# One core, a transformer block with product-key experts: the last eight modulation sums stand in other chunks of the expert phase, and the blocks of the gate matrix G are spread over fewer halves

## The chip, the core and the metric

The kernel runs on one core of a Trainium2 chip, in one launch. The metric is the device time of that launch in microseconds (us); of several runs the median counts.

## What is computed

The program runs two blocks on 256 tokens of width 1024. The change lies in the expert layer of the first block and in one of the vectors that it is gated with:

```python
def adaln_params(cond, w_mod, b_mod):
    mod = jax.nn.silu(cond) @ w_mod + b_mod
    return mod.reshape(cond.shape[0], N_MOD, 1, cond.shape[-1])
...
        u = expert_u[experts]
        vsel = expert_v[experts]
        act = jax.nn.gelu(jnp.einsum('thkd,td->thk', u, hb), approximate=False)
        return jnp.einsum('thk,thkd->td', gate * act, vsel)
...
        x = x + mod[:, 5] * peer_ffn(h2, peer_w_query[layer], peer_sub_keys[layer], peer_u[layer], peer_v[layer])
```

There are 16,384 experts, and each token chooses 8 x 16 of them. The kernel gathers nothing: it multiplies all tokens with all experts, and a matrix G, with the gate of each pair of token and expert (zero where the token did not choose the expert), weighs the result before the second product.

## The kernel before

**Chunks and halves.** All large weights come as 257 chunks of 1 MB, one after the other, into three buffers `raw`. A chunk has two halves of 128 x 1024. Each half is split in two fp32r parts: ScalarE (ACT) copies it to `w_hi`, VectorE (DVE) subtracts to get `w_lo` (a helper records both, at lines 1399 and 1827), and TensorE (PE) multiplies three times with the pair (line 868). There are four slots for pairs, and both ACT and DVE split up to three halves ahead of the one that PE is to start (`ahead`). SyncE (SP) issues in one queue, in program order: chunk n only when both halves of chunk n-3 have been read by DVE.

**The expert phase.** 64 chunks U and 64 chunks V. First come U(0) to U(35), 72 halves h = 0 to 71, alone. Then a loop over c = 0 to 63 runs V(c), and from c = 34 to 61 U(c+2) ahead of it. U(c) is finished by a gelu on ACT. Before V(c), DVE multiplies the gelu's result by G (`weigh(c)`, output `wfull`), ACT rounds that to `HC` (`w_high`), DVE makes the rest (`weighed_low`, again `HC`). DVE's iteration c is: `weighed_low(c+1)`, splits of U(c+2) if there is one, `weigh(c+2)`, a split, `one_hots` of block 36+c (for c < 28), a modulation sum if it stands here, a split.

**G's blocks.** G is made in two rounds of 32 blocks of 8 tokens. For block n DVE writes one-hot rows (`one_hots(n)`, five operations, after PE has finished block n-2), PE multiplies them (`g_block(n)`, 24 matmuls of 128x64), ACT copies the result (`g_copy(n)`). The first round, blocks 0 to 31, runs beside the U halves: NG = 42, so they follow the halves h = 30 to 71, block 31 right after the last half. `weigh(0)` needs all 32 of them. Blocks 32 and 33 follow the last half, and block 34+c stands at V(c) for c < 30. Block 32 may be copied only once `weigh(0)` has read G, block 33 after `weigh(1)`.

**The eight modulation sums.** The vector mod[:, 5] is made of the blocks 40 to 47 (`GATE2`). Each is one operation on DVE over 128x1024 (`mod_block`, line 1984) on a piece of `w_mod` of 0.5 MB that lies in `x`, which is free at that time. `gate2_at(n)` says in which c it stands: 28, 30, ..., 42. SP asks for the piece of block n ahead of the chunk V(c) of that c (lines 835 to 837); as there is one buffer, it first waits until the sum of block n-1 is done (`summed`), and whatever stands behind in SP's queue waits too. V(28) is chunk 96, V(30) chunk 98; from c = 34 on there are two chunks for each c. The finished vector is turned by PE at c = 48, goes through DRAM and is read in the norm behind V(63); `x` is brought back from DRAM from chunk V(48) on.

**Reloads.** The gelu results of U(8) to U(35) are kept in DRAM and reloaded one for each V chunk (0.25 MB, lines 847 and 855). SP waits for the landing of one before it issues the next.

Of the kernel before, what the change touches and what calls it, by code (L numbers as in the profile page):

```python
# [28 lines left out]
NBL = 256 // TB  # L29
# [58 lines left out]

NU = 36
NG = 42  # L90


KEPT = range(8, NU)
# [3 lines left out]
def blocks_after(h):  # L97

    j = h - (2 * NU - NG)
    return range(NBL * j // NG, NBL * (j + 1) // NG) if j >= 0 else range(0)  # L100

PEER_U, PEER_V = {}, {}

# [135 lines left out]

def gate2_at(n):  # L240

    return 28 + 2 * (n - GATE2[0])


def mod_issue():


    at, u = {}, 0
    for s in FRONT:
        if s in HALF_OF:  # L250
            u = HALF_OF[s]
        elif s[0] == "mod":
            at[s] = u
    out, chunk = {}, 0
    for n in range(NMOD, GATE2[0]):
        before = HALF_OF["win", 0, 2] if n < NMOD + 4 else at["mod", n - 4]
        chunk = max(chunk, (before + 9) // 2)
        out.setdefault(chunk, []).append(n)
    for n in GATE2:
        out.setdefault(PEER_V[gate2_at(n)] // 2, []).append(n)  # L260
    return out


# [124 lines left out]
def program(nc, wall, keys_d, cols_d, rows_d, bigrows_d, crow_d, wmod_d, dist_d, x_d, ctx_d, pT_d, gws_d, out_d, n_chunks):  # L388
    assert n_chunks * 2 == U_END
    with ExitStack() as es:  # L390
# [409 lines left out]
        def sync_program(e):  # L800
            e.dma_start(cols[:, :], cols_d).then_inc(s_tab, 16)
            e.dma_start(crow_ctx, crow_d[1024:2048].partition_broadcast(128)).then_inc(s_crow, 16)
            e.dma_start(crow, crow_d[0:1024].partition_broadcast(128)).then_inc(s_crow, 16)
            for n in range(n_chunks):
                if n == 1:
                    e.dma_start(x[:, :, :], x_d.rearrange("(i p) d -> p i d", p=128)).then_inc(s_x, 16)
                if n == 2:
                    e.dma_start(ctx, ctx_d.rearrange("(i p) d -> p i d", p=128)).then_inc(s_ctx, 16)
                if n == 6:
                    e.dma_start(rows[:, :], rows_d.partition_broadcast(128)).then_inc(s_tab, 16)  # L810
                if n == 10:
                    e.wait_ge(s_tab, 32)
                    e.dma_start(dist, dist_d.rearrange("p (a b) -> p a b", a=4)).then_inc(s_tab, 16)
                if n == 11:
                    e.wait_ge(s_c2, 3)
                    e.dma_start(crow_keep.rearrange("(p d) -> p d", p=1), crow[0:1, :]).then_inc(s_ckeep, 16)
                if n == U_QUERY // 2:
                    e.wait_ge(s_pt_, 8)
                    e.dma_start(skeep, keys_d).then_inc(s_keys, 16)
                if n == U_QUERY // 2 + 4:  # L820
                    e.wait_ge(s_res, result(N_PEER, 1, 1))
                    e.dma_start(x_keep, x[:, :, :].rearrange("p i d -> p (i d)")).then_inc(s_xkeep, 16)
                if n == PEER_V[48] // 2:
                    e.wait_ge(*summed(GATE2[7]))
                    e.dma_start(x[:, :, :].rearrange("p i d -> p (i d)"), x_keep).then_inc(s_xback, 16)
                for m in MOD_ISSUE.get(n, []):
                    place, times = mod_slot(m)
                    if m < NMOD + 4:
                        e.wait_ge(*summed(7))
                        e.wait_ge(s_std, 2)  # L830
                    elif m == GATE2[0]:
                        e.wait_ge(s_w, 24)
                        e.wait_ge(s_ckeep, 16)
                        e.dma_start(crow2, crow_keep.partition_broadcast(128)).then_inc(s_rawm[4], 16)
                    else:
                        e.wait_ge(*summed(m - (1 if m in GATE2 else 4)))
                    e.dma_start(mod_raw[place], wmod_d[m - NMOD]).then_inc(s_rawm[place], 16)
                if n >= NRAW:
                    for u in (2 * (n - NRAW), 2 * (n - NRAW) + 1):
                        e.wait_ge(*read(u))  # L840
                e.dma_start(raw[:, n % NRAW, :], wall[n]).then_inc(s_raw[n % NRAW], 16)
                if n in ACTS_OUT:
                    c = ACTS_OUT[n]
                    e.wait_ge(s_gelu, c + 1)
                    if c > KEPT[0]:
                        e.wait_ge(s_ao, kept(c - 1))
                    e.dma_start(act_keep[c - KEPT[0]], act_made(c)).then_inc(s_ao, 16)
                if n in ACTS_IN:
                    c = ACTS_IN[n]
                    e.wait_ge(s_ao, kept(KEPT[-1]))  # L850
                    if c > KEPT[0]:
                        e.wait_ge(s_ai, kept(c - 1))
                    if c >= KEPT[4]:
                        e.wait_ge(s_w, c - 3)
                    e.dma_start(act_of(c), act_keep[c - KEPT[0]]).then_inc(s_ai, 16)
            for i in range(2):
                for hf in range(2):
                    s_ = slice(hf * 512, (hf + 1) * 512)
                    e.wait_ge(s_fin, 2 * i + hf + 1)
                    e.dma_start(out_d[i * 128:(i + 1) * 128, s_], gt[:, i, s_]).then_inc(s_out, 16)  # L860
            e.wait_ge(s_out, 64)


        def tensor_program(e):
# [333 lines left out]
            for h in range(2 * NU):  # L1198
# [3 lines left out]
                    turn_choice(1, sel)  # L1202
                for b in blocks_after(h):
                    g_block(b)
            for b in (NBL, NBL + 1):
                g_block(b)
            for c in range(64):
                if NU <= c + 2 < 64:
                    for m in range(2):
                        u_half(c + 2, m)  # L1210
                if c == 48:
                    t.wait_ge(s_gc, NQ * NBL)
                    gate_turned(GATE2[0])
                if NBL + 2 + c < NQ * NBL:
                    g_block(NBL + 2 + c)
                if c < 62:
                    for m in range(2):
                        for i in range(2):
                            ins = tok_half(PEER_V[c] + m, i, [0, 1, 2, 3], lambda i: weighed(c, m, i), c == m == 0, False)
                        t.did(ins, s_used)  # L1220
# [168 lines left out]
        def scalar_program(e):  # L1389
# [252 lines left out]
            def w_high(c):  # L1642
                a.wait_ge(s_w, c + 1)
                if c >= 2:
                    a.wait_ge(s_used, used(PEER_V[c - 2] + 1))
                act(WR[:, c % 2, 0, :], wfull, ACT.Copy, sig=s_wh)

            for h in range(2 * NU):
# [8 lines left out]
                        act(gsel, gsel, ACT.Exp, sig=s_ge)  # L1657
                for b in blocks_after(h):
                    g_copy(b)
            w_high(0)  # L1660
            for b in (NBL, NBL + 1):
                g_copy(b)
            for c in range(64):
                if c < 63:
                    w_high(c + 1)
                if NU <= c + 2 < 64:
                    for m in range(2):
                        ahead(PEER_U[c + 2] + m)
                    a.wait_ge(s_w, c + 1)
                    gelu(c + 2)  # L1670
                if c < 63:
                    ahead(PEER_V[c])
                if NBL + 2 + c < NQ * NBL:
                    g_copy(NBL + 2 + c)
                if c < 62:
                    ahead(PEER_V[c] + 1)
                if c == 48:
                    a.wait_ge(s_gtn, 2)
                    act(gT, PB[6][0:8, 0:128], ACT.Copy, sig=s_gcp)
            norm(N_F1, PEER_V[63] + 1, f_scr)  # L1680
# [139 lines left out]
        def vector_program(e):  # L1820
# [470 lines left out]
            def weighed_low(c):  # L2291
                v.wait_ge(s_wh, c + 1)
                tt(WR[:, c % 2, 1, :], wfull, WR[:, c % 2, 0, :].bitcast(F32), SUB, sig=s_wl)
# [3 lines left out]
            for h in range(2 * NU - NG, 2 * NU):  # L2297
                for b in blocks_after(h - 1):
                    one_hots(b + 2)
                ahead(U_PEER + h)  # L2300
            for b in blocks_after(2 * NU - 1):
                one_hots(b + 2)
            weigh(0)
            weighed_low(0)
            weigh(1)
            for n in range(NBL + 2, NBL + 4):
                one_hots(n)
            mods_at = {gate2_at(n): n for n in GATE2}
            for c in range(64):
                if c < 63:  # L2310
                    weighed_low(c + 1)
                if NU <= c + 2 < 64:
                    for m in range(2):
                        ahead(PEER_U[c + 2] + m)
                if c + 2 < 64:
                    weigh(c + 2)
                if c < 63:
                    ahead(PEER_V[c])
                if NBL + 4 + c < NQ * NBL:
                    one_hots(NBL + 4 + c)  # L2320
                if c in mods_at:
                    mod_block(mods_at[c])
                if c == 46:
                    added_mods(GATE2[0], 48)
                if c < 62:
                    ahead(PEER_V[c] + 1)
# [390 lines left out]
```

## Time and profile before

| | us |
|---|---|
| median of three runs | 1788.83 |
| the three runs | 1788.52 to 1795.13 |
| the profiled execution, its own time | 1793.46 |
| its span, first to last instruction | 1791.7 |
| PE busy | 1666.4 (93%) |
| DVE busy | 1254.2 (70%) |
| ACT busy | 909.8 (51%) |

Below, a row of a timeline gives the start, the duration, the engine and the operation, and in square brackets how long the engine had stood idle before it and what ended that. A row can stand for several operations in a row (x5), and small gaps lie in its duration. PE is shown busy until the modelled end of a matmul, so its pace is read from the starts of rows that come again, not from its busy share. The granted clock is 1 at 2.4 GHz and 0.5 at 1.2 GHz. The expert phase ends near 1153 us.

### The profile page before, as it was taken

The page shows a single profiled execution, that of the slowest core. Times are in us where ns is not written, and L with a number is a line of the kernel's source. Part 1 is how long each engine was busy: PE and PEld are TensorE (multiplying, and loading weights), DVE is VectorE, ACT ScalarE, POOL GpSimd, SP SyncE. Part 2 cuts the span into 40 slices and gives each one's busy share as a digit, 9 for nine tenths or more (in the row PEclk, how much of TensorE's full clock was granted, in tenths as well). Part 3 has the DMA queues.
Part 4 walks back from the last instruction along what each step waited for, and adds up shares of the span by engine and source line. Part 5 has one row for each costly group of instructions (what it writes and reads, how often), then busy time and mean ns, then how long its engine had stood idle before and what let it go on. Part 6 is the DMA issues. An engine that isn't in the chain of part 4 may idle for free.

```text
span 1791.7 us, 29060 instructions
## 1 busy us (share of the span) xinstructions
PE 1666.4 (93%) x11518; PEld 1492.9 (83%) x11518; DVE 1254.2 (70%) x2040; ACT 909.8 (51%) x1206; POOL 84.2 (5%) x50
## 2 busy tenths in 40 slices
PE   6898787999999899988999999999998888999996
PEld 6676566998999788867999999899998777899995
DVE  5886655899888899976666555665556885655555
ACT  3454445554555455534444444544446766544445
POOL 1100002622000000000000000000000000000000
PEclk9898888999999999999999999999999998999998
DMA  6743333446655355637555555454543532555541
GB/s 262 275 168 133 106 110 123 144 165 200 205 182 199 141 201 202 220 133 267 211 199 211 198 189 186 154 200 177 191 185 130 212 130 106 190 193 188 188 171 64
DMA packets 53418, 318.52 MB, mean 178 GB/s; under 512 B 5953, under 2 KB 6113, under 8 KB 19362
## 3 DMA queue, kind: packets, MB, share of 16 engines
q1 hardware_dynamic: 52098, 310.60, 48.7%
q0 software_dynamic: 1184, 6.05, 0.9%
q8 instruction: 91, 1.49, 0.3%
q14 instruction: 45, 0.37, 0.1%
HBM read 307.17 MB, written 9.47 MB: 177 GB/s over the span
## 4 chain that ended last, share of the span: by engine, by line
PE 61%; DVE 25%; ACT 10%; issue 2%; DMA 2%; DVEq 0%; SPq 0%; ACTq 0%
PE pb L868 60%; DVE w_lo L1827 7%; DVE ar L1827 7%; ACT w_hi L1399 4%; ACT ar L1399 3%; DVE ar L1839 2%; DMA raw<-in_wall 1%; DVE HC L1827 1%; DVE ar L2181 1%; ACT L1399 1%; ACT HC L1399 1%; DVE ar L2178 1%; DVE ar L1984 1%; DVE raw L1984 1%; DVE ar L1981 1%
## 5 line engine op out<-in xcount | busy, mean ns | idle before, releaser
L1827 DVE TENSOR_TENSOR w_lo<-raw,w_hi 128x1024 fp32r<-128x1024 f32 x467 | 572.3, 1225 | 277.3 <-ACT w_hi L1399 251.8
L868 PE MATMUL pb<-HX,w_hi 128*128 128x256 f32 x3904 | 716.7, 285 | 12.2 <-DVE w_lo L1827 10.7
L1399 ACT ACTIVATE w_hi<-raw 128x1024 fp32r<-128x1024 f32 x498 | 528.2, 1061 | 346.2 <-PE pb L868 297.9
L868 PEld LDWEIGHTS pb<-HX,w_hi 128*128 128x128 f32 x3904 | 614.0, 193 | 19.7 <-DVE w_lo L1827 10.3
L868 PE MATMUL pb<-HX,w_lo 128*128 128x256 f32 x1952 | 553.9, 284 | 0.0
L868 PE MATMUL pb<-w_hi,HC 128*128 128x512 f32 (+1 forms) x1648 | 530.8, 393 | 11.7 <-DVE HC L1827 11.2
L868 PEld LDWEIGHTS pb<-HX,w_lo 128*128 128x128 f32 x1952 | 375.9, 193 | 0.0
L868 PEld LDWEIGHTS pb<-w_hi,HC 128*128 128x128 f32 x1648 | 312.0, 190 | 76.4 <-DVE w_lo L1827 12.5
L868 PE MATMUL pb<-w_lo,HC 128*128 128x512 f32 (+1 forms) x824 | 322.4, 391 | 0.0
L1827 DVE TENSOR_TENSOR ar<-ar 128x512 bf16<-128x512 bf16 (+8 forms) x470 | 247.5, 563 | 59.3 <-ACT ar L1399 30.9
L1399 ACT ACTIVATE ar<-pb 128x512 f32<-128x512 f32 (+3 forms) x203 | 112.7, 555 | 242.6 <-PE pb L868 154.9
L868 PE MATMUL pb<-w_hi,HX 128*128 128x512 f32 x512 | 177.7, 416 | 13.2 <-DVE w_lo L1827 5.6
L868 PEld LDWEIGHTS pb<-w_lo,HC 128*128 128x128 f32 x824 | 156.6, 190 | 29.4
L868 PE MATMUL pb<-ar 128*128 128x64 bf16 (+3 forms) x1960 | 134.1, 228 | 26.4 <-DVE ar L1827 8.7
L868 PEld LDWEIGHTS pb<-ar 128*128 128x128 bf16 (+2 forms) x1960 | 111.7, 124 | 50.7 <-issue 26.8
L868 PEld LDWEIGHTS pb<-w_hi,HX 128*128 128x128 f32 x512 | 102.4, 200 | 38.2 <-issue 11.4
L1399 ACT ACTIVATE HC<-ar 128x512 fp32r<-128x512 f32 x87 | 55.0, 632 | 103.8 <-PE pb L868 60.7
L868 PE MATMUL pb<-w_lo,HX 128*128 128x512 f32 x256 | 104.4, 408 | 0.0
L1827 DVE TENSOR_TENSOR HC<-ar,HC 128x512 fp32r<-128x512 f32 x87 | 60.3, 693 | 46.6 <-ACT HC L1399 42.8
L2565 POOL TENSOR_TENSOR w_lo<-raw,w_hi 128x1024 fp32r<-128x1024 f32 x31 | 75.7, 2442 | 158.5 <-ACT w_hi L1399 117.9
L1399 ACT ACTIVATE ar<-ar 128x512 f32<-128x512 f32 (+7 forms) x85 | 50.3, 591 | 57.5 <-DVE ar L1839 23.8
L868 PEld LDWEIGHTS pb<-w_lo,HX 128*128 128x128 f32 x256 | 51.3, 201 | 9.7
(139 smaller groups left out, 716.1 us busy)
## 6 DMA issues: line engine op xcount, KB each, us to landing
raw<-in_wall SPq DMA_DIRECT2D x257, 1024.0 KB, 4.8
ar<-in_wmod SPq DMA_DIRECT2D x24, 512.0 KB, 3.7
act_keep<-ar SPq DMA_DIRECT2D x28, 256.0 KB, 5.6
ar<-act_keep SPq DMA_DIRECT2D x28, 256.0 KB, 5.1
x<-in_wmod SPq DMA_DIRECT2D x8, 512.0 KB, 3.3
ar<-in_bigrows POOLq DMA_DIRECT2D x2, 1024.0 KB, 5.1
ar<-acs_keep POOLq DMA_DIRECT2D x2, 1024.0 KB, 8.4
ar<-in_crow SPq DMA_DIRECT2D x2, 512.0 KB, 5.9
```

The lines of the kernel that those rows point to most:

```text
L868: return e.matmul(o, l, r, start=start, stop=stop, skip_group_check=True)
L1399: a.did(e.activation(out, in_, func, scale=scale, **kw), sig)
L1827: v.did(e.tensor_tensor(out, a_, b_, op), sig)
L1839: v.did(e.scalar_tensor_tensor(out, a_, s_, b_, op0, op1), sig)
L1981: v.did(e.scalar_tensor_tensor(junk, w, 1.0, crow_ctx, MUL, MUL, accum_out=modT[:, n, 1:2]))
L1984: v.did(e.scalar_tensor_tensor(w, w, 1.0, c_, MUL, MUL, accum_out=modT[:, n, 0:1]), s_modv)
L2178: v.did(e.max(vals[:, c_], src))
L2181: v.did(e.max_index(idx[:, c_], vals[:, c_], src))
L2565: p.did(e.tensor_tensor(w_lo[:, made % NH, :], raw_half(w), w_hi[:, made % NH, :].bitcast(F32), SUB), s_lop)
```

## The change

Three things change.

1. `gate2_at` gives c = 34, 36, ..., 48 in place of 28, 30, ..., 42, and the piece of block n is asked for one chunk later than V(c)'s own (in the chunk of U(c+3), which follows V(c)). What hangs on the last sum moves by six: the bias is added at c = 52 (46 before), the turn stands at c = 54 (48), `x` comes back from V(54) on.
2. Blocks 0 to 31 are spread over 38 halves in place of 42, h = 30 to 67. The halves 68 to 71 have none of them.
3. Work that stood behind the last U half stands beside it: `weigh(0)` at h = 69, `weighed_low(0)`, `weigh(1)`, `one_hots(34)`, `w_high(0)` and the blocks 32 and 33 at h = 70. `one_hots(35)` follows h = 71.

```diff
+U_LAST = 2 * NU - 1
...
-    return range(NBL * j // NG, NBL * (j + 1) // NG) if j >= 0 else range(0)
+    return range(min(NBL, NBL * j // (NG - 4)), min(NBL, NBL * (j + 1) // (NG - 4))) if j >= 0 else range(0)
...
-    return 28 + 2 * (n - GATE2[0])
+    return 34 + 2 * (n - GATE2[0])
...
-        out.setdefault(PEER_V[gate2_at(n)] // 2, []).append(n)
+        out.setdefault(PEER_V[gate2_at(n)] // 2 + 1, []).append(n)
...
-                if n == PEER_V[48] // 2:
+                if n == PEER_V[54] // 2:
...
-            for b in (NBL, NBL + 1):
-                g_block(b)
+                if h == U_LAST - 1:
+                    for b in (NBL, NBL + 1):
+                        g_block(b)
...
-                if c == 48:
+                if c == 54:
                     t.wait_ge(s_gc, NQ * NBL)
                     gate_turned(GATE2[0])
...
-            w_high(0)
-            for b in (NBL, NBL + 1):
-                g_copy(b)
+                if h == U_LAST - 1:
+                    w_high(0)
+                    for b in (NBL, NBL + 1):
+                        g_copy(b)
...
-            for b in blocks_after(2 * NU - 1):
-                one_hots(b + 2)
-            weigh(0)
-            weighed_low(0)
-            weigh(1)
-            for n in range(NBL + 2, NBL + 4):
-                one_hots(n)
+                if h == U_LAST - 2:
+                    weigh(0)
+                if h == U_LAST - 1:
+                    weighed_low(0)
+                    weigh(1)
+                    one_hots(NBL + 2)
+            one_hots(NBL + 3)
...
-                if c == 46:
+                if c == 52:
                     added_mods(GATE2[0], 48)
```

SP's queue in the stretch V(28) to V(33), before: a piece of `w_mod` (`in_wmod`) ahead of chunks 96, 98, 100 and 103. `in_wall` is a chunk, `act_keep` a reload.

```order
L834 DMA x<-crow_keep 128x1024
L837 DMA x<-in_wmod 128x1024
L841 DMA raw<-in_wall 128x2048
L855 DMA ar<-act_keep 128x512
L841 DMA raw<-in_wall 128x2048
L855 DMA ar<-act_keep 128x512
L837 DMA x<-in_wmod 128x1024
L841 DMA raw<-in_wall 128x2048
L855 DMA ar<-act_keep 128x512
L841 DMA raw<-in_wall 128x2048
L855 DMA ar<-act_keep 128x512
L837 DMA x<-in_wmod 128x1024
```

The same queue now, from chunk 100 on:

```order
L842 DMA raw<-in_wall 128x2048
L856 DMA ar<-act_keep 128x512
L842 DMA raw<-in_wall 128x2048 x2
L856 DMA ar<-act_keep 128x512
L835 DMA x<-crow_keep 128x1024
L838 DMA x<-in_wmod 128x1024
L842 DMA raw<-in_wall 128x2048 x4
L838 DMA x<-in_wmod 128x1024
L842 DMA raw<-in_wall 128x2048 x4
```

The first piece now stands ahead of chunk 104, behind the last reload, and each next one four chunks on.

DVE at the end of the U halves, before. `ar<-ar 128x512` followed by `128x1024` and three more `128x512` is one `one_hots`; a `128x512` more is a `weigh`; `HC` is `weighed_low`.

```order
L1827 TENSOR_TENSOR w_lo<-raw,w_hi 128x1024
L1827 TENSOR_TENSOR ar<-ar 128x512
L1827 TENSOR_TENSOR ar<-ar 128x1024
L1827 TENSOR_TENSOR ar<-ar 128x512 x4
L1827 TENSOR_TENSOR HC<-ar,HC 128x512
L1827 TENSOR_TENSOR ar<-ar 128x512 x2
L1827 TENSOR_TENSOR ar<-ar 128x1024
L1827 TENSOR_TENSOR ar<-ar 128x512 x4
L1827 TENSOR_TENSOR ar<-ar 128x1024
L1827 TENSOR_TENSOR ar<-ar 128x512 x3
L1827 TENSOR_TENSOR HC<-ar,HC 128x512
```

DVE there now, from the splits at h = 68 and 69 on:

```order
L1830 TENSOR_TENSOR w_lo<-raw,w_hi 128x1024 x2
L1830 TENSOR_TENSOR ar<-ar 128x512
L1830 TENSOR_TENSOR w_lo<-raw,w_hi 128x1024
L1830 TENSOR_TENSOR HC<-ar,HC 128x512
L1830 TENSOR_TENSOR ar<-ar 128x512 x2
L1830 TENSOR_TENSOR ar<-ar 128x1024
L1830 TENSOR_TENSOR ar<-ar 128x512 x3
L1830 TENSOR_TENSOR w_lo<-raw,w_hi 128x1024
L1830 TENSOR_TENSOR ar<-ar 128x512
L1830 TENSOR_TENSOR ar<-ar 128x1024
L1830 TENSOR_TENSOR ar<-ar 128x512 x3
L1830 TENSOR_TENSOR HC<-ar,HC 128x512
```

The two `weigh` and the first `weighed_low` now have three splits among them, and the last split before V(0) stands between `one_hots(34)` and `one_hots(35)`. No operation is added or taken away on any engine.

## Rows read from the trace of the kernel before

**Rows 1.** The chain that ended last, in time: start, us, what
```profile
786.41 5.43 DMA raw<-in_wall
```
**Rows 2.** Stretches: us, busy PE, PEld, DVE, ACT, POOL; PE clock, DMA share, GB/s
```profile
588.00:598.00 10.00, 4.05 (x101) 3.83 (x100) 8.55 (x17) 4.71 (x7) 0.00 (x0) 0.82 0.26 104
...
780.00:830.00 50.00, 37.03 (x177) 29.85 (x175) 28.58 (x32) 17.65 (x21) 0.00 (x0) 0.90 0.53 205
...
795.00:799.00 4.00, 3.88 (x9) 3.13 (x10) 3.16 (x4) 2.91 (x4) 0.00 (x0) 0.50 0.08 24
...
812.00:816.00 4.00, 3.35 (x9) 2.66 (x10) 3.69 (x4) 3.03 (x4) 0.00 (x0) 0.62 0.87 309
```
**Rows 3.** Timeline of V(28) to V(33), DVE and SP
```profile
781.78 0.69 DVE L1827 TENSOR_TENSOR HC<-ar,HC 128x512 fp32r<-128x512 f32 x1
...
784.72 1.23 DVE L1984 SCALAR_TENSOR_TENSOR x<-x 128x1024 f32<-128x1024 f32 x1
...
785.98 0.33 SPq L837 DMA_DIRECT2D x<-in_wmod  x1
...
792.55 0.33 SPq L855 DMA_DIRECT2D ar<-act_keep  x1
```
**Rows 4.** Timeline of PE, V(28) to V(34)
```profile
776.13 0.47 PE L868 MATMUL pb<-w_hi,HC 128*128 128x512 f32 x1
...
781.70 0.90 PE L868 MATMUL pb<-ar 128*128 128x64 bf16 x24
782.62 0.47 PE L868 MATMUL pb<-w_hi,HC 128*128 128x512 f32 x1
...
795.12 0.77 PE L868 MATMUL pb<-w_hi,HC 128*128 128x512 f32 x1 [6.82 <-DVE HC L1827]
...
812.65 0.51 PE L868 MATMUL pb<-w_hi,HC 128*128 128x512 f32 x1 [4.41 <-DVE HC L1827]
...
830.10 0.50 PE L868 MATMUL pb<-HX,w_hi 128*128 128x256 f32 x2 [1.82 <-DVE w_lo L1827]
...
833.07 0.40 PE L868 MATMUL pb<-w_hi,HC 128*128 128x512 f32 x1
```
**Rows 5.** Waits from 832 to 1160 us: engine <- releaser: total us, times, longest
```profile
PE pb L1078 <- DVE x L1827: 2.6, 3, 1.5
```
**Rows 6.** Timeline of PE, U halves with a block after them
```profile
542.75 0.90 PE L868 MATMUL pb<-ar 128*128 128x64 bf16 x24
...
549.33 0.90 PE L868 MATMUL pb<-ar 128*128 128x64 bf16 x24
...
553.02 0.90 PE L868 MATMUL pb<-ar 128*128 128x64 bf16 x24
```
**Rows 7.** Timeline of DVE, U halves 67 to 71
```profile
576.29 1.23 DVE L1827 TENSOR_TENSOR w_lo<-raw,w_hi 128x1024 fp32r<-128x1024 f32 x1 [1.19 <-ACT w_hi L1399]
578.18 2.16 DVE L1827 TENSOR_TENSOR ar<-ar 128x512 bf16<-128x512 bf16 x5 [0.67 <-PE pb L868]
...
585.57 2.16 DVE L1827 TENSOR_TENSOR ar<-ar 128x512 bf16<-128x512 bf16 x5 [0.21 <-PE pb L868]
```
**Rows 8.** Timeline of PE and DVE, last U half to V(1)
```profile
588.33 1.63 PE L868 MATMUL pb<-ar 128*128 128x64 bf16 x48
...
591.52 0.89 PE L868 MATMUL pb<-ar 128*128 128x64 bf16 x24 [1.57 <-DVE ar L1827]
...
596.79 1.44 PE L868 MATMUL pb<-ar 128*128 128x64 bf16 x24 [4.38 <-DVE ar L1827]
598.04 0.77 PE L868 MATMUL pb<-w_hi,HC 128*128 128x512 f32 x1
...
599.05 0.69 DVE L1827 TENSOR_TENSOR HC<-ar,HC 128x512 fp32r<-128x512 f32 x1
...
605.85 0.47 PE L868 MATMUL pb<-w_hi,HC 128*128 128x512 f32 x1
...
605.97 0.69 DVE L1827 TENSOR_TENSOR HC<-ar,HC 128x512 fp32r<-128x512 f32 x1 [0.51 <-ACT HC L1399]
```

More of the change, by code:

```diff
@@ L1676, in scalar_program @@
                     ahead(PEER_V[c] + 1)
-                if c == 48:
+                if c == 54:
                     a.wait_ge(s_gtn, 2)
```

## Prediction

> **What bounds the kernel now.** I read the chain of waits first, then the busy time by stretches, then the timelines around each place where PE stands idle. PE is busy 93% of the span, so only the places where it is not can give time back. In the expert phase there are two.
>
> The first is V(28) to V(34). In the 50 us from 780 PE is busy 37.03 us, at a mean clock of 0.90 [rows 2]. It stands idle 6.82 us ahead of V(30), 4.41 ahead of V(32) and 1.82 inside U(36) [rows 4]. The chain runs there through a chunk's transfer that starts at 786.41 and takes 5.43 us [rows 1]. SP's queue tells why it starts so late: the sum of block 40 ends near 786, and at 785.98 SP issues the next piece of w_mod, with chunk 98 right behind [rows 3]. Without that wait, chunk 98 would have been issued when chunk 95 was read, and that is over two V chunks earlier. So the wait for a sum, which stands in front of a chunk in an in-order queue, is what holds PE. Behind 832 us PE waits on nothing but three short waits of the norm's rows, 2.6 us in all [rows 5], although five of the eight sums stand there.
>
> The second is the step from U to V. The last U half ends at 588.33; PE then does blocks 31 and 32, waits 1.57 us, does block 33, waits 4.38, does block 34 and starts V(0) at 598.04 [rows 8], in a stretch where it is busy 4.05 of 10 us [rows 2]. What it waits for is DVE, which has `weigh(0)`, `weighed_low(0)`, `weigh(1)` and two `one_hots` to do one after the other.
>
> **Pace of PE and DVE between them.** A U half with a block takes 553.02 - 549.33 = 3.69 us, two halves with one block 549.33 - 542.75 = 6.58; so a half is 2.89 and a block 0.80 [rows 6]. V(1) starts at 605.85 [rows 8] and V(28) at 776.13 [rows 4]: 170.28 / 27 = 6.307 us a chunk, without idle time. DVE's `weighed_low(2)` starts at 605.97 [rows 8] and `weighed_low(29)` at 781.78 [rows 3]: 175.81 / 27 = 6.511. DVE is the slower one by 0.204 a chunk, but starts with a lead. `weighed_low(c+1)` may start up to 5.65 us after V(c) (781.78 - 776.13); at c = 1 it starts 0.12 after, at c = 28 the lead is gone, and V(29) starts at 782.62, as soon as `weighed_low(29)` is done (781.78 + 0.84). The start of V(29) is therefore set by PE and by DVE at once: moving PE's start of V alone would gain nothing. The transition is worth what DVE gains.
>
> **Part 1, the step from U to V.** PE: the last U half now has blocks 31, 32 and 33 ahead of it in addition, 3 x 0.80, and ends at 590.7; block 34 follows, and V(0) could start at 591.5, 6.5 earlier than now. DVE: counting back from 590.7 by halves of 2.89 and two blocks, U half 69 ends at 583.3 on PE. ACT then does a gelu (0.6) and the copy of half 73 (1.06; both from the durations of its line on the page), so DVE gets that half at 585.0, and this is its last wait. What it then has to do, with a gap of 0.10 behind each (split 1.23 and `one_hots` 2.16 in [rows 7], `weighed_low` 0.69 in [rows 8], and `weigh` of the same shape): split 1.33, `weighed_low(0)` 0.8, `weigh(1)` 0.8, `one_hots(34)` 2.26, split 1.33, `one_hots(35)` 2.26, together 8.8. `weighed_low(1)` starts at 593.8 (599.05 now), and one iteration of 6.51 later `weighed_low(2)` at 600.3 against 605.97. DVE gains 5.7 us. At c = 1 it is 600.3 - 597.8 = 2.5 behind V(1), so its lead is used up near c = 1 + (5.65 - 2.5) / 0.204 = 16, and from there it paces. V(29) starts at 600.3 + 27 x 6.511 + 0.84 = 776.9 in place of 782.62. **5.7 us** gained, of the 6.5 plus the slow first 3 us of V(0) that PE alone would have.
>
> Where does DVE's time come from? Halves without a block cost it 1.19 + 0.67 = 1.86 us of waiting, halves with one 0.21 [rows 7]. Four of ten such halves go from the spread to the end, and there `weigh` and the rest stand in them. That the blocks are closer costs PE nothing: a half with a block is 3.69 us for PE and 1.33 + 2.26 = 3.59 for DVE.
>
> **Part 2, the sums.** From V(29) to V(34) there are now 833.07 - 782.62 = 50.45 us [rows 4]. The work in it is five V chunks without a block, 776.13 to 781.70, thus 5.57 each, and the two halves of U(36): 27.85 + 5.8 = 33.6. The rest, 16.8 us, is 13.05 of idle time and 3.8 of matmuls at the lower clock behind it (795 to 799 stands at 0.50, the 1.2 GHz level, 812 to 816 at 0.62) [rows 2]. With no piece asked for in that stretch SP is held by nothing but reads. DVE needs 2 x 1.33 + 2 x 0.8 = 4.3 us a chunk there against PE's 5.57, and so gets its lead back. **16.8 us** gained.
>
> The Trainium skill ("TensorE: Matmul & The Clock Gate", Part 1) says that the array is throttled by default and activity releases it, and that the penalty is the throttled time times one minus the ratio. An estimate by that page from the granted clock of the two stretches is 3.88 x 0.50 + 3.35 x 0.38 = 3.2 us in place of my 3.8, and the sum would be 0.6 smaller.
>
> **What the moved sums cost where they now stand.** Eight sums of 1.33 us lie beside U and V chunks, one in each second c. There DVE has 4 splits, `weigh`, `weighed_low` and a sum in 11.3 us of PE: 5.3 + 1.6 + 1.3 = 8.2. The five that stand there already cost PE nothing [rows 5]. The request for a piece is in front of chunk 104 + 4i, and the sum it waits for is done when DVE has read chunk 100 + 4i and before it reads 101 + 4i; chunk 104 + 4i can't be issued before 101 + 4i is read, so SP never waits for the sum where it counts. A piece has four chunks to land. Queued behind that request are its own chunk and nothing else, the reloads having ended with chunk 102. The copy of the row and the piece, 1 MB in all, come before chunk 104, once. Turn, way through DRAM and return of `x` start six c later, with nine c (100 us) left to the norm: 0. Nothing in `gate2_at` touches POOL but through that turn.
>
> **Sum.** 5.7 + 16.8 = 22.5 us. The profiled execution, 1793.46, would become 1771.0; it stands 4.6 above the median of the runs, which would become 1788.83 - 22.5 = **1766.3**.
>
> **Rivals.**
>
> B, DVE gains nothing at the step. Its margin in the U halves is 0.1 us a half (3.59 against 3.69). If the closer blocks make it late, V(29) stays where it is, and only part 2 is left: 1788.8 - 16.8 = 1772.0. For it: two values 3% apart. Against: six light halves stay among the 38, each with 1.86 us to catch up.
>
> C, the reloads pace V(28) to V(33). SP waits for one to land before it issues the next; between about 786.9, right behind the chunk of [rows 1], and the next issue at 792.55 [rows 3] lie 5.67 us, and with 0.45 for issuing 6.1 against PE's 5.57. Six chunks would give back 3.2 us: 1769.5. Against: that transfer shared the queue with a piece and two chunks, and DVE and the buffers are two chunks ahead. The mean of 205 GB/s at a share of 0.53 [rows 2] means that 237 GB/s (1.31 MB in 5.57 us) fill 0.61 of the engines.
>
> D, the sums stall the mixed stretch (slower). Seven requests wait for the sum before them. Three cost 16.8 us where they were, 5.6 each; if a sum came later than the read of the chunk before by more than a chunk's spare time, some 5 us, seven would cost 39, and the time would be 1766.3 + 39 = 1805. Against it stands [rows 5]: the same requests one chunk earlier cost nothing.
>
> E, the 13 us idle have a second cause (a reload or buffer that comes late anyway). Then only part 1 is left: 1788.8 - 5.7 = 1783.1.
>
> F, PE sets V's pace throughout, because DVE comes out earlier than I count: V(29) at 597.8 + 28 x 6.307 = 774.4, 8.2 gained at the step: 1763.8.
>
> **Numbers.** Forecast 0.68, B 0.12, C 0.08, D 0.03, E 0.04, F 0.05. The range reaches from F less 1.5 of spread among runs to B with the same, 1762 to 1773.5. Half a per cent is 8.9 us, about what a measurement of this kernel can tell from no change: faster by more are the forecast, B, C and F, 0.93; E is within it, 0.04; D is slower, 0.03.
>
> **What would show it.** In the profile of the changed kernel: V(0) within 1 us of the last U half, at full clock; `weighed_low(2)` near 600; PE's V chunks 6.31 apart up to about V(16) and 6.51 apart behind it, up to V(29) near 777; no idle time over 1 us from there to V(34), which starts near 810 in place of 833.07; SP's waits for a sum with no PE wait beside them. The prediction is wrong if PE waits behind a block in the halves 30 to 71, if V(30) to V(33) are over 5.7 apart, or if a wait for a split stands near a sum.

## Result and profile after

The changed kernel takes 1774.4 us in the median of four runs (1771.53 to 1776.26), and the kernel before, in four runs of which three are the ones above, 1791.98 (1788.52 to 1796.58). The ratio is 0.9889, with a 95% interval of 0.987 to 0.9908. Put on the 1788.83 that I started from, that is 1769.0 us (1765.6 to 1772.4); the median itself lies 0.9 us above the range of 1762 to 1773.5, because more runs moved the kernel before up from 1788.8 to 1792, and to 1793.9 to 1795.4 in the later comparisons. Forecast was a gain of 22.5 us; the three comparisons of the changed kernel give 19.9, 21.0 and 21.4, and the span of the profiled execution fell by 21.9, from 1791.7 to 1769.8.

The page of the changed kernel, the chain that ended last:

```profile
PE 73%; DVE 17%; ACT 7%; issue 1%; DMA 1%; SPq 0%; DVEq 0%; ACTq 0%
```

Busy times are what they were (PE 1665.2 us, DVE 1254.4, ACT 910.0); PE's share of the chain that ended last has grown to 73% (61% on the page of before), and that of the DMA has fallen to 1% (2%).

The step from U to V, timeline of PE, which answers to [rows 8]:

```profile
582.89 1.63 PE L869 MATMUL pb<-ar 128*128 128x64 bf16 x48
...
587.31 0.90 PE L869 MATMUL pb<-ar 128*128 128x64 bf16 x24
588.04 0.48 PE L869 MATMUL pb<-w_hi,HC 128*128 128x512 f32 x1
```

Blocks 32 and 33 stand ahead of the last U half, block 34 right behind it, V(0) behind that, at full clock (0.48 and not 0.77 us for its first matmul) and without a wait. The same place on DVE, its `weighed_low(1)` and `(2)`:

```profile
590.70 0.69 DVE L1830 TENSOR_TENSOR HC<-ar,HC 128x512 fp32r<-128x512 f32 x1
...
597.22 0.69 DVE L1830 TENSOR_TENSOR HC<-ar,HC 128x512 fp32r<-128x512 f32 x1
```

They are 6.52 us apart (6.92 in the kernel before, with the idle 0.51 of [rows 8], in which DVE waits for ACT). V(1) starts at 594.33, so DVE is 2.9 us behind it at c = 1 (2.5 forecast). How that goes on is seen in the chain, start, us and what:

```profile
579.93 109.26 PE pb L869 x890
689.27 6.46 PE pb L869 x48
...
773.96 257.59 PE pb L869 x1608
```

Up to 689 us, the end of V(15), PE is in one piece, at 6.31 us a chunk (V(15) itself starts 6.43 behind V(14)); behind that each V chunk is a piece of its own, 6.52 us apart, and starts when its `weighed_low`, 5.68 us behind the start of the chunk before, is done; and from V(29) on, at 773.96, the chain is PE alone for 257 us. In the kernel before a chunk's transfer stood in that place [rows 1].

The stretches that answer to those of [rows 2], same columns, the V(29) to V(34) stretch in the second:

```profile
586.00:596.00 10.00, 10.00 (x92) 8.55 (x91) 9.20 (x18) 6.25 (x8) 0.00 (x0) 1.00 0.35 101
773.00:823.00 50.00, 49.92 (x286) 43.35 (x286) 38.80 (x39) 27.00 (x30) 0.00 (x0) 1.00 0.70 249
```

PE is busy 49.92 of 50 us in place of 37.03, at clock 1.00 in place of 0.90, and the DMA engines move 249 GB/s at a share of 0.70. SP in the same stretch asks for its first piece at 791.89 and the second at 811.64, and no PE wait stands beside them. What SP waited for a sum from 770 to 1000 us, in all, times and longest, in the kernel before and in the changed one:

```profile
SPq L837 <- DVE x L1984: 65.5, 7, 19.7
```
```profile
SPq L838 <- DVE x L1987: 6.6, 7, 1.0
```

The seven waits are still there, but short. For all of 832 to 1160 us PE's waits are again three for the norm's rows, 2.6 us in all.

### The profile page after: what moved, and what is told of

Same layout as the page of the kernel before. It is cut to its first block, busy times and chain, and to the rows that moved or that the text cites. A ratio compares the mean times of both kernels' runs of the same rounds, so it can differ in the third digit from the quotient of the medians.

```text
span 1769.8 us, 29060 instructions
## 1 busy us (share of the span) xinstructions
PE 1665.2 (94%) x11518; PEld 1493.6 (84%) x11518; DVE 1254.4 (71%) x2040; ACT 910.0 (51%) x1206; POOL 84.7 (5%) x50
## 4 chain that ended last, share of the span: by engine, by line
PE 73%; DVE 17%; ACT 7%; issue 1%; DMA 1%; SPq 0%; DVEq 0%; ACTq 0%
PE pb L869 72%; DVE w_lo L1830 4%; DVE ar L1830 3%; ACT ar L1401 3%; DVE ar L1842 2%; ACT w_hi L1401 2%; DVE ar L2184 1%; ACT L1401 1%; DMA raw<-in_wall 1%; DVE ar L1987 1%; DVE ar L2181 1%; DVE raw L1987 1%; DVE ar L1984 1%; ACT HX L1401 1%; DVE ar L2188 0%
## 5 line engine op out<-in xcount | busy, mean ns | idle before, releaser
L869 PE MATMUL pb<-w_hi,HC 128*128 128x512 f32 (+1 forms) x1648 | 525.3, 390 | 2.3 <-DVE HC L1842 1.2
```

The source lines that it names most:

```text
L869: return e.matmul(o, l, r, start=start, stop=stop, skip_group_check=True)
```

## Experiments

All numbers of the next table are starts read from the profiled execution's timeline of PE. T is the last of the six matmuls that turn the chosen experts, ahead of the first block; what the expectations call the end of the queries is this point, 0.54 us behind the start of their row. The last column is a stage of the second block that no edit touches, from PE's matmul 9000 to 10000 of 11518.

| kernel | T to V(0) | V(0) to V(1) | V(1) to V(29) | V(29) to V(34) | V(34) to V(48) | untouched stage |
|---|---|---|---|---|---|---|
| before | 159.5 | 7.8 | 176.8 | 50.4 | 157.1 | 201.9 |
| before_again | 158.0 | 7.3 | 176.9 | 50.5 | 157.1 | 203.6 |
| after | 151.4 | 6.3 | 179.6 | 33.0 | 157.1 | 206.0 |
| after_again | 152.9 | 6.3 | 179.5 | 33.1 | 157.1 | 203.4 |
| after_third | 151.4 | 6.3 | 179.6 | 33.0 | 157.1 | 205.9 |
| mods_only | 158.0 | 7.2 | 177.0 | 33.0 | 157.1 | 203.7 |
| blocks_only | 151.4 | 6.3 | 179.6 | 51.4 | 157.3 | 203.8 |
| ask_later | 158.0 | 7.3 | 176.8 | 33.2 | 157.1 | 203.7 |
| ask_early | 151.4 | 6.3 | 179.5 | 33.0 | 174.6 | 205.5 |
| spread_only | 155.7 | 8.4 | 176.7 | 51.8 | 157.1 | 203.6 |
| pool_five | 152.9 | 6.3 | 182.8 | 33.0 | 157.1 | 199.4 |
| fuller | 152.9 | 6.3 | 176.8 | 33.0 | 157.1 | 203.6 |

**before_again and after_again: what two traces of one kernel differ by.** No edit.

> The kernel before, unchanged, against itself. Theory (run spread): the ratio is 1.000 and its interval tells what can be told apart, some 3 us either way. In its profile the stretch from V(29) to V(34) takes 50.4 us again (50.45 in the first trace) and V(0) to V(29) 184.6 again, within 0.5, since they are set by waits that don't depend on the clock's phase; the front (up to 440 us) and the mixer behind 1340 us may differ by 2 to 5 us, because the granted clock falls at other places there. Rival (the change did something behind 1340 us): those two differ by under 1 us between two traces of the same kernel, and then the 4 us that the changed kernel gave back between 1345 and 1490 us are its own.

> The changed kernel, unchanged. Ratio 0.988 to 0.990 again. In its profile V(0) starts within 1 us of the last U half, V(29) to V(34) takes 33.0 us within 0.3, PE's V chunks are 6.31 us apart up to about V(14) and 6.51 behind it. Theory (run spread): the stage behind 1340 us comes out 1 to 4 us other than in the first trace of the changed kernel. Rival (the change costs something there): it is as long as in the first trace, within 0.5 us.

Ratios 0.9996 (0.9986 to 1.0005) and 0.9883 (0.9869 to 0.9897). V(29) to V(34) came again within 0.1 us in both kernels. The untouched stage took 201.9 and 203.6 us in two traces of the kernel before and 206.0, 203.4 and 205.9 in three of the changed kernel. One kernel's own traces thus differ there by up to 2.6 us, less than the 4 us that the changed kernel seemed to give back behind 1340 us; but before_again and after_again have 203.6 and 203.4, and among all traces of the table, in which this stage has the same code, it takes 199.4 to 206.0. The 4 us are no effect of the change, and the rival falls. The stretch in after and in after_again, as busy time by stretch:

```profile
1316.00:1522.00 206.00, 188.67 (x1002) 161.96 (x1001) 146.43 (x213) 130.57 (x182) 4.31 (x7) 0.92 0.40 147
```
```profile
1320.00:1524.00 204.00, 184.58 (x1004) 158.00 (x1004) 146.49 (x214) 131.01 (x182) 4.32 (x7) 0.94 0.41 150
```

The longer one has the lower clock, 0.92 against 0.94, and 4.1 us more of busy PE, with the same DVE and ACT work. The 1.5 us by which T to V(0) differs between after and after_again are of that kind too: the 40 us from 441 have a mean clock of 1.00 in the one and those from 443 a mean of 0.96 in the other.

**mods_only: part 2 alone.** The kernel before with

```diff
-    return 28 + 2 * (n - GATE2[0])
+    return 34 + 2 * (n - GATE2[0])
...
-        out.setdefault(PEER_V[gate2_at(n)] // 2, []).append(n)
+        out.setdefault(PEER_V[gate2_at(n)] // 2 + 1, []).append(n)
```

and what hangs on it at 54 and 52.

> Only the sums are moved (c = 34 to 48, asked for one chunk on); the blocks and the step from U to V are as before. Theory (SP's wait for a sum holds the chunks): V(29) starts where it does in the kernel before, V(29) to V(34) takes 33.0 us in place of 50.4, gain 17.4 us, ratio 0.990. Rival (the two parts are not additive, the sums' stretch would need DVE's lead from the other part): DVE comes into V(28) with no lead here as in both kernels, so the gain would be under 14 us, with PE waits of over 1 us ahead of V(30) or V(31).

V(29) to V(34) took 33.04 us, 17.4 less; ratio 0.9912 (0.9898 to 0.9927), 15.8 us (13 to 18). DVE has no lead at V(28) here either, and PE did not wait. The first theory holds.

**blocks_only: part 1 and the spread alone.** The changed kernel with the lines of mods_only turned back.

> Only the blocks and the step from U to V are changed; the sums stand at c = 28 to 42 and are asked for as before. Theory (the step is worth what DVE gains): V(0) starts about 10 us earlier than before relative to a common point in the U halves' beginning, but V(29) only 5.7 to 7 us earlier, the stretch V(29) to V(34) is 50.4 us again, ratio 0.9965. Rival (the two gains overlap, as DVE reaches V(28) just as late and the stall swallows the rest): under 3 us, ratio over 0.998. Rival (PE's start counts): 9 us or more.

T to V(29) took 337.2 us against 342.2 in before_again: 5.0 gained, as much as DVE gains (its `weighed_low(2)` starts 160.5 us behind T, 165.5 in before_again). V(0) comes 6.6 earlier, not about 10. At V(1) it is 7.7 (165.3 against 157.7), and 2.7 are given back up to V(29), because DVE then sets the pace. The stretch behind it took 51.35, 0.9 more, so 4.1 are left in the profile. Timed: 0.9985 (0.9977 to 0.9994), 2.7 us (1.1 to 4.1); the 0.9965 expected lies outside, and the number that came is that of the first rival (under 3 us, over 0.998). Its mechanism is not what the trace shows, for V(29) comes 5.0 earlier; but that was under the 5.7 to 7 expected, and not all of it passed the stall. Here is the stretch from V(29) to V(34) in before_again, in blocks_only and, of an experiment further down, in spread_only; in the changed kernel the same matmuls are busy 33.04 us, at clock 1.00:

```profile
782.25:832.73 50.48, 36.88 (x169) 30.52 (x170) 29.05 (x31) 18.75 (x21) 0.00 (x0) 0.90 0.56 214
```
```profile
775.62:826.97 51.35, 37.65 (x168) 31.37 (x169) 30.30 (x32) 18.74 (x21) 0.00 (x0) 0.90 0.57 220
```
```profile
779.82:831.60 51.78, 39.31 (x169) 32.60 (x169) 30.45 (x32) 18.74 (x21) 0.00 (x0) 0.87 0.57 219
```

PE's idle time is 13.6 us in before_again and 13.7 here. Nearly all of the 0.9 is in the matmuls themselves: at the waits the clock falls to its 1.2 GHz level for a while (0.50 from 795 to 799 us in [rows 2]), and how much work falls into that while differs (one trace each).

**ask_later: the sums stay, only the request moves.** One line of the kernel before:

```diff
-        out.setdefault(PEER_V[gate2_at(n)] // 2, []).append(n)
+        out.setdefault(PEER_V[gate2_at(n)] // 2 + 2, []).append(n)
```

> The kernel before with one edit: each piece is asked for two chunks later; the sums stay at c = 28 to 42. Theory (the in-order wait in SP's queue is the cause, not where DVE does the sums): the sum waited for is then done 1.3 us after the chunk could go anyway, so V(29) to V(34) takes 33.0 to 34.5 us in place of 50.4 (33.04 with the sums moved), ratio 0.991. DVE has the sum's 1.33 us in V(28), V(30), V(32) on top of 4.3 us, against PE's 5.45. Rival (the sums' own time on DVE, which reaches V(28) without a lead, holds PE): 3 x 1.3 us and more of waits stay, over 37 us. Rival (the piece lands too late for its sum): DVE waits for a piece ahead of a sum, and PE behind it.

V(29) to V(34) took 33.2 us, ratio 0.9904 (0.9886 to 0.9922). This one line gives what mods_only gives, and neither rival came. The timeline of DVE and SP around the first sum shows why:

```profile
785.02 1.22 DVE L1984 SCALAR_TENSOR_TENSOR x<-x 128x1024 f32<-128x1024 f32 x1
```
```profile
771.97 0.33 SPq L841 DMA_DIRECT2D raw<-in_wall  x1
...
778.47 0.33 SPq L841 DMA_DIRECT2D raw<-in_wall  x1
...
786.28 0.33 SPq L837 DMA_DIRECT2D x<-in_wmod  x1
786.71 0.38 SPq L841 DMA_DIRECT2D raw<-in_wall  x1
```

The sum ends and SP asks for the next piece as in [rows 3], but chunks 98 and 99 had left the queue ahead of the wait, at 771.97 and 778.47. In the kernel before both stood behind it. So it is neither the sum nor its place on DVE, but what stands behind the wait in SP's queue.

**ask_early: the same wait put back where the sums now are.** The changed kernel with

```diff
-        out.setdefault(PEER_V[gate2_at(n)] // 2 + 1, []).append(n)
+        out.setdefault(PEER_V[gate2_at(n)] // 2 - 2, []).append(n)
```

> The changed kernel with one edit: the pieces are asked for two chunks ahead of V(c), not one behind it; the sums stay at c = 34 to 48. Theory (a chunk queued behind a sum costs what the path chunk, copy, split, 8.7 us from the end of the sum, takes beyond what PE has split ahead, some 7.3 us in the mixed stretch): seven waits of about 1.4 us, V(34) to V(48) 157.1 + 10 = 167 us (160 to 180). V(29) to V(34) stays at 33.0. Rival (the mixed stretch is immune): 157.1 again.

V(34) to V(48) took 174.6 us, 17.5 more, in the range but above the 10 worked out; the one time was 1788.13 us. PE waited seven times for a split, 12.5 us in all. The first of the seven, on DVE, SP and PE:

```profile
809.95 1.23 DVE L1987 SCALAR_TENSOR_TENSOR x<-x 128x1024 f32<-128x1024 f32 x1
...
811.21 0.33 SPq L838 DMA_DIRECT2D x<-in_wmod  x1
...
818.27 1.23 DVE L1830 TENSOR_TENSOR w_lo<-raw,w_hi 128x1024 fp32r<-128x1024 f32 x1 [7.09 <-ACT w_hi L1401]
819.55 0.50 PE L869 MATMUL pb<-w_hi,HC 128*128 128x512 f32 x1 [1.60 <-DVE w_lo L1830]
```

From the end of the sum to PE's start are 8.4 us: issue, landing, copy, split. Five of the seven waits are as forecast (1.4 to 1.7, and 1.4 worked out); the fourth and the fifth are 2.6 and 2.4, as from the issue of the chunk to ACT's copy 6.5 and 6.3 us pass there and 5.6 in the first (811.63 to 817.18). What I had left out is what follows the waits: PE's busy time from V(34) to V(48) is 162.1 us in place of 157.1. Of these 5.0 us some 3.3 are the clock, which stands at 0.50 from 893.2 to 896.6 and from 920.5 to 923.9, at the two longest waits; the rest is 0.2 to 0.3 us behind each of the seven. So the intervals of two c are 22.44 us without a wait, 24.1 to 24.4 with a short one and 26.7 with each of these two.

**spread_only: the closer blocks without the rest.** The kernel before with the line of `blocks_after` alone.

> The kernel before with one edit: blocks 0 to 31 over 38 halves; the step from U to V stands behind the last half as before, and so do the sums. Theory (the step is worth what DVE gains, and DVE gains only if work stands in the halves that are left empty): from the end of the queries (438.4 us in the traces) to V(29) 342.2 us in the kernel before, 337.2 with both edits; here 2.4 less than 342.2, so 339.8. The ratio is 0.998 to 0.999. Rival (closer blocks alone give all of it): 337.2. Rival (they cost PE or DVE something in the U halves): over 342.2.

T to V(29) took 340.9 us, 1.3 less, and V(29) to V(34) 1.3 more, all of it in busy PE at a lower mean clock (the rows at blocks_only: PE idle 12.5 us there, busy 39.31); ratio 0.9995 (0.9985 to 1.0005). That V(29) would gain 2.4 was too much: V(0) comes 2.3 earlier but `weighed_low(2)` and V(1) only 1.2, and PE waits 3.8 us for `one_hots(34)`. Closer blocks mainly empty the last halves; most of the gain is in the work that is put there (3.7 of the 5.0 us).

**pool_five: taking five splits off DVE.** The changed kernel with

```diff
+LO_POOL |= {PEER_V[c] + 1 for c in (4, 8, 12, 16, 20)}
...
-            ahead(PEER_U[15] + 1)
+            ahead(PEER_V[20] + 1)
```

> The changed kernel with one edit: GpSimd (POOL) subtracts five of the V halves, the second ones of V(4), V(8), V(12), V(16), V(20), in place of DVE. Theory (DVE paces V(14) to V(29), at 6.51 us a chunk against PE's 6.307): DVE has 1.33 us less five times, more than the 3.0 us by which it falls behind, so the chunks are 6.31 us apart up to V(29), and from V(1) to V(29) it is 28 x 6.307 = 176.6 us in place of 179.6; the kernel is 3 us shorter, ratio to the kernel before 0.9866. Rival (POOL's subtraction, 2.4 us on the page, comes too late or slows DVE's operations beside it): waits of PE for POOL, 179.6 or more.

V(1) to V(29) took 182.8 us, 3.3 more; ratio 0.9894 (0.987 to 0.9918). The rival came true. Timeline of POOL and DVE at the first of the five:

```profile
614.23 1.23 DVE L1831 TENSOR_TENSOR w_lo<-raw,w_hi 128x1024 fp32r<-128x1024 f32 x1
614.29 3.42 POOL L2569 TENSOR_TENSOR w_lo<-raw,w_hi 128x1024 fp32r<-128x1024 f32 x1 [196.19 <-ACT w_hi L1402]
615.56 2.70 DVE L1831 TENSOR_TENSOR HC<-ar,HC 128x512 fp32r<-128x512 f32 x1
```

POOL's subtraction takes 3.42 us here and `weighed_low` beside it 2.70 in place of 0.69. DVE is spared 1.33 us and loses 2.01, and as `weighed_low` is what PE waits for, PE waits four times 1.3 us. The rows read as if the two engines took turns: in all five places POOL's subtraction ends 2.2 to 2.3 us after DVE's split beside it has ended (615.46 and 617.71 above), and `weighed_low` 0.5 to 0.6 us after POOL's (618.26). That reads as waiting, on both engines, and not as slower work. The Trainium skill ("GPSIMD Engine Reference", Specifications) says that GpSimd shares its SBUF interfaces with VectorE, with contention for DVE instructions that have two SBUF inputs; this one has two, and the trace agrees.

**fuller: more of DVE's work in the U halves.** The changed kernel with these lines; what goes with them on PE, on ACT and in DVE's loop over c is left out here:

```diff
-    return range(min(NBL, NBL * j // (NG - 4)), min(NBL, NBL * (j + 1) // (NG - 4))) if j >= 0 else range(0)
+    return range(min(NBL, NBL * j // (NG - 6)), min(NBL, NBL * (j + 1) // (NG - 6))) if j >= 0 else range(0)
...
-                if h == U_LAST - 2:
+                if h == U_LAST - 4:
                     weigh(0)
-                if h == U_LAST - 1:
+                if h == U_LAST - 3:
                     weighed_low(0)
                     weigh(1)
                     one_hots(NBL + 2)
-            one_hots(NBL + 3)
+                if h == U_LAST - 2:
+                    one_hots(NBL + 3)
+                if h == U_LAST - 1:
+                    weighed_low(1)
+                    weigh(2)
```

> The changed kernel carried on: blocks 0 to 31 over 36 halves, weigh(0) at h = 67, weighed_low(0), weigh(1), blocks 32 and 33 at h = 68, one_hots(35) at h = 69, and weighed_low(1), weigh(2) and w_high(1) at h = 70, so that more of DVE's work lies in the U halves, where it waits for PE, and weighed_low(2) can start with V(1). Theory (V(1) to V(29) takes 179.5 us in the changed kernel in place of 28 x 6.307 = 176.6 because DVE starts it with too small a lead): 176.6 to 177, V(0) no later in relation to the U halves, 3.0 us less in all; ratio to the kernel before 0.9865. Rival (DVE's pace in V is bound by something that a lead doesn't help): 6.51 us a chunk from V(14) on again. Rival (DVE becomes late in the U halves): PE waits for a split or a block between 450 and 588 us.

> The changed kernel once more, on the same chip as the version carried on. V(1) to V(29) 179.5 us, V(29) to V(34) 33.05, ratio 0.988.

V(1) to V(29) took 176.8 us, 2.8 less than in the changed kernel, so PE is its own bound up to V(28). T to V(0) is 152.9, as in after_again; the 1.5 more than in after_third are clock again (0.96 in the 40 us from 441). The times on one chip are 1769.25 us against 1773.46, ratios 0.9857 (0.984 to 0.9873) and 0.9881 (0.9864 to 0.9897). The intervals overlap; that it is faster rests on the 2.8 us of the trace and on four runs that all lie below the four of the other (1769.0 to 1769.5, 1772.8 to 1773.6). It is the best version of this study.

## Why the prediction was right, point by point

- **The wait in SP's queue.** Right, and shown from three sides: taken out with the sums moved (33.0 us), taken out with the sums in place (33.2), put back elsewhere (17.5 us lost). The gain was forecast at 16.8 and measured at 17.4, as V(29) to V(33) take 5.46 us each in the mean and not 5.57; my 5.57 was read from V(28), which follows a block. In the terms of my sum that is 13.05 of idle time and 4.4 of slower matmuls, not 3.8. By the rule on the clock's share from the Trainium skill ("TensorE: Matmul & The Clock Gate", Part 1) it would have been 16.2, further off. The fault there was my choice of two windows of 4 us: over all of the low clock in which PE works (795.12 to 799.28 and 812.94 to 816.35, 7.57 us at 0.50) an estimate by the same rule gives 3.8 in place of 3.2.
- **The step from U to V is worth what DVE gains.** Right in its mechanism: V(1) comes 7.7 us earlier, `weighed_low(2)` 5.0, and V(29) 5.0. The size was forecast at 5.7 (T to V(29) is 342.2 against 337.2). About half of the miss is DVE's end, 2.9 us behind V(1) and not 2.5. The other half is the trace I counted from, in which `weighed_low(2)` is 6.92 us behind `weighed_low(1)`, with 0.51 of idle time at a low clock [rows 8]; in before_again it is 6.51. The 1.5 us more of slow clock ahead of V(0) in that trace shift both ends of my sum alike.
- **The switch of the bound.** Forecast near V(16), seen at V(15); V(29) is set by DVE at 6.52 us a chunk. fuller shows that the lead is what was missing.
- **Moved sums cost nothing.** Right: 157.1 us in both kernels from V(34) to V(48).
- **Sum.** 5.0 + 17.4 = 22.4 in the traces against 22.5: the two misses, 0.7 too much and 0.6 too little, cancel, and that the sum comes out to 0.1 is luck. Timed it is 19.9 to 21.4, with intervals that reach from 16.5 to 24.4 and all hold 22.4.
- **Rivals.** Neither B nor F occurred, as the step gained 5.0 us, not 0 or 8.2; in fuller, another kernel, PE sets V's pace as F has it. C didn't occur: V(29) to V(33) follow each other at 5.44 to 5.52 us with the reloads in the queue. D's mechanism exists, but its price is 2.5 us a request in the mixed stretch (ask_early) and not the 5.6 that I took from the pure V chunks; I put that down to the U chunk more of split work that PE has there, which no run separates. E fell with mods_only.
- **The base.** The median of my three runs, 1788.83, was 5 us below what 23 runs gave later (1793.9), the single runs reaching from 1788.5 to 1797.6, and I took 1.5 us for the spread among runs. That, and not the mechanism, put the median of the changed kernel 0.9 us outside the range.

## What to carry to other kernels

A wait placed in front of a request in a queue that issues in order holds everything behind it: put the request as many places back as its data can spare, and the wait costs nothing, without moving any work (here two chunks of 1 MB sufficed). Where two engines pace a loop within a few per cent of each other, a gain at the loop's entrance counts only as far as the slower one gets it, so fill the idle places of that engine ahead of the loop. A gain ahead of a stretch that still stalls need not come through whole, because the slow clock behind the waits can fall on more work (0.9 and 1.3 us here), so parts measured alone need not add up.

## What the runs showed of the hardware

- A subtraction of POOL over 128x1024, both inputs in SBUF, held a DVE subtraction over 128x512 of the same kind for 2.0 us (0.69 to 2.70), and itself took 3.42 us, 2.44 in the mean of the kernel before; five times out of five the rows look like turns taken whole.
- The same matmuls (V(29) to V(34)) are busy 33.04 us at a granted clock of 1.00 and 36.9 to 39.3 us in stretches with three waits of 1.8 to 6.8 us, at means of 0.90 to 0.87.
- Two traces of one kernel differ by up to 2.6 us in a stage of 204 us, at mean clocks of 0.92 and 0.94, and by 1.5 us from T to V(0), with 0.96 and 1.00 in 40 us of it; twelve traces with the same code in that stage reach from 199.4 to 206.0 us.
